# Windowed means as band matrices on TensorE behind the group's matrix, and token-major products in 512 columns

## The reference, cut to what matters

```python
def multiscale_pool_mixer(x, pool_w, pool_scale):     # POOL_WINDOWS = (2, 4, 8, 16), one for each group of 256 channels
    xg = x.astype(jnp.float32).reshape(B, S, POOL_GROUPS, POOL_CH)
    cs = jnp.cumsum(xg, axis=1)
    for gi, w in enumerate(POOL_WINDOWS):
        c = cs[:, :, gi]
        lagged = jnp.pad(c, ((0, 0), (w, 0), (0, 0)))[:, :S]
        mean = (c - lagged) / jnp.minimum(pos, float(w))[:, None]
        feats.append(mean - xg[:, :, gi])
    p = jnp.stack(feats, axis=2).astype(x.dtype)
    y = jnp.einsum('bsgc,gcd->bsgd', p, pool_w).reshape(B, S, D_MODEL)
    return y * pool_scale
# values of the linear attentions, of the memory attention and of the window attention
h = x @ w_in; i_v = split(h)            # (512 x 1024) @ (1024 x 512)
v = (mem_n @ w_v)                       # (256 x 1024) @ (1024 x 1024), in each of two layers
v = split(h2 @ w_in_2)                  # (512 x 1024) @ (1024 x 1024)
k, v = jnp.split(rmsnorm(h2, kv_norm) @ w_kv, 2, axis=-1)   # v: 128 columns, shared by all heads
```

## Time and profile before

| | us |
|---|---|
| median of 3 runs (lowest, highest) | 2575.34 (2572.87, 2576.18) |
| the profiled execution, its own time | 2575.22 |
| its span, first to last instruction | 2573.4 |
| PE busy | 2477.0 (96%) |
| DVE busy | 1482.1 (58%) |
| ACT busy | 879.1 (34%) |
| mean granted TensorE clock | 0.983 of 2.4 GHz |

### The profile page before, as it was taken

One profiled execution on the slowest core, in us unless ns is written; L12 is line 12 of the kernel. 1 busy time (PEld: TensorE's weight loads), 2 busy tenths in 40 slices (PEclk: granted clock), 3 DMA queues, 4 the chain that ended last, 5 costly groups with the idle time before them and its releaser, 6 DMA issues.

```text
span 2573.4 us, 29864 instructions
## 1 busy us (share of the span) xinstructions
PE 2477.0 (96%) x11776; PEld 2028.1 (79%) x11776; DVE 1482.1 (58%) x2044; ACT 879.1 (34%) x1184; POOL 9.9 (0%) x23
## 2 busy tenths in 40 slices
PE   8999999999999799999998999999999999999998
PEld 7898777788887577788886788778888777788886
DVE  6888645544446845544446535566666666566666
ACT  3444543422223543422224434322222455322222
POOL 0000000000000000000000000000000000000000
PEclk9998999999999799999999999999999999999999
DMA  5222211322222121222222220232222111222221
GB/s 189 82 83 82 99 66 66 115 95 91 93 96 89 58 82 66 82 98 98 96 91 80 82 99 33 68 117 96 98 98 98 66 66 50 91 92 96 97 98 65
DMA packets 32815, 225.56 MB, mean 88 GB/s; under 512 B 3765, under 2 KB 3813, under 8 KB 6368
## 3 DMA queue, kind: packets, MB, share of 16 engines
q1 hardware_dynamic: 31536, 220.21, 25.1%
q0 software_dynamic: 1200, 4.23, 0.5%
HBM read 222.30 MB, written 2.12 MB: 87 GB/s over the span
## 4 chain that ended last, share of the span: by engine, by line
PE 86%; DVE 8%; ACT 4%; issue 1%; DMA 0%; DVEq 0%; SPq 0%; ACTq 0%
PE bank L644 85%; DVE w_lo L1733 2%; ACT w_hi L1232 1%; ACT xs L1291 1%; DVE xs L1816 1%; DVE cacc L1924 1%; ACT xh L1245 1%; DVE hs L1975 0%; DVE xs L1830 0%; PE bank L1183 0%; DVE xs L1785 0%; DVE xl L1741 0%; DVE gs L1975 0%; PE bank L912 0%; DVE sum_x L1752 0%
## 5 line engine op out<-in xcount | busy, mean ns | idle before, releaser
L644 PE MATMUL bank<-xh,w_hi 128*128 128x512 f32 x1976 | 787.5, 399 | 58.0 <-DVE xl L1741 22.2
L644 PE MATMUL bank<-xl,w_hi 128*128 128x512 f32 x1976 | 777.2, 393 | 0.0
L644 PE MATMUL bank<-xh,w_lo 128*128 128x512 f32 x1976 | 776.9, 393 | 0.0
L1733 DVE TENSOR_TENSOR w_lo<-w_raw,w_hi 128x2048 fp32r<-128x2048 f32 x205 | 469.6, 2291 | 403.0 <-ACT w_hi L1232 402.4
L1232 ACT ACTIVATE w_hi<-w_raw 128x2048 fp32r<-128x2048 f32 x205 | 391.3, 1909 | 372.9 <-PE bank L644 372.7
L644 PEld LDWEIGHTS bank<-xh,w_hi 128*128 128x128 f32 x1976 | 375.9, 190 | 156.1 <-issue 34.8
L644 PEld LDWEIGHTS bank<-xh,w_lo 128*128 128x128 f32 x1976 | 375.6, 190 | 80.0
L644 PEld LDWEIGHTS bank<-xl,w_hi 128*128 128x128 f32 x1976 | 376.2, 190 | 78.7 <-issue 2.2
L1785 DVE TENSOR_TENSOR xs<-xs,bank 128x512 f32<-128x512 f32 x448 | 294.2, 683 | 116.3 <-PE bank L644 115.3
L644 PE MATMUL bank<-mhh,w_lo 128*128 128x512 f32 x512 | 199.2, 389 | 0.0
L644 PE MATMUL bank<-mhh,w_hi 128*128 128x512 f32 x512 | 199.2, 389 | 0.0
(11 more groups left out here) (282 smaller groups left out, 2688.2 us busy)
## 6 DMA issues: line engine op xcount, KB each, us to landing
w_raw<-weights_in SPq DMA_DIRECT2D x205, 1024.0 KB, 5.0
xs<-x_in SPq DMA_DIRECT2D x4, 512.0 KB, 8.0
sf<-rel_scratch POOLq DMA_DIRECT2D x1, 2048.0 KB, 11.7
y_out<-xs SPq DMA_DIRECT2D x8, 256.0 KB, 2.0
w_raw<-weights_in SPq DMA_DIRECT2D x2, 512.0 KB, 6.7
mk<-mem_in POOLq DMA_DIRECT2D x1, 1024.0 KB, 9.2
sum_q<-consts_in POOLq DMA_DIRECT2D x1, 256.0 KB, 9.4
scan<-consts_in POOLq DMA_DIRECT2D x1, 256.0 KB, 3.1
```

Source lines behind the costliest of these rows:

```text
L644: return pe.matmul(dst, a, b, start=start, stop=stop)
L1733: dve.tensor_tensor(w_lo[:, c % 2, :], w_raw[:, c % 2, :], w_hi[:, c % 2, :].bitcast(F32), ALU.subtract)\
```

## The change

1. **Pooling behind the matrix.** The windowed mean minus identity and the group's matrix commute. PE now multiplies first, token-major: `pool_values(g)` makes, from the split tiles of the group, 24 fp32r matmuls of 256 columns into two banks (`z`); ACT drains them to `zt`. `pool_means(g)` then makes for each of the group's two output tiles, in plain fp32, 4 matmuls of 128 columns (a tile of 128 tokens of `zt` stationary, a 128 x 128 band matrix streaming) and 3 of 16 columns for the window's reach over the next tile. The band matrices (`window`, 1152 columns of constants) replace `invpos`. DVE's `pool` and ACT's copies to `pa` go; DVE splits and evicts only. `mixn1`'s sums come from running sums on DVE in place of PE's ones-matmuls for six tiles.
2. **Token units in 512 columns.** `token_half` replaces `token_unit`: a unit holds 512 columns of half of the features, two units make a product. Each token tile has a bank of its own from the first half to the end of the second. This goes for `v`, `mv0`, `mv1a`, `mv1b`, `gv`. Drains come after the second half: the filler's at k = 4 alone.
3. **Statistics by token.** The one-column sums go. For `r0` PE transposes `rstd` by 4 matmuls against a column of the identity, behind `gq`'s second unit. For `r2` nothing is left: `sv` is made feature-major (24 matmuls of 512 columns), DVE multiplies it by `rstd` into `vf`, PE transposes it into bank 6 behind `sq`'s first unit, ACT drains it.

```diff
+    def token_pair(stage, p, tiles):
+        n = UNITS[stage] + 2 * p + 1
+        for t in range(tiles):
+            fill((stage, p, t), t if tiles == TT else 2 * (p % 2) + t, n if t == tiles - 1 else None)
...
+            def token_half(stage, p, half, src, tiles):
+                c = UNITS[stage] + 2 * p + half
+                pe.wait_ge(w_lo_ready, c + 1)
+                for t in range(tiles):
+                    key = (stage, p, t)
+                    if half == 0:
+                        wait_free(pe, key)
+                    for k in range(KT // 2):
+                        h, l = src(KT // 2 * half + k)
+                        last = mm3(bank(key)[:, :], (h[:, t * P:(t + 1) * P], l[:, t * P:(t + 1) * P]),
+                                   weights(c, k * T, T), half == 0 and k == 0, half == 1 and k == KT // 2 - 1)
+                    if half == 1:
+                        full(last, key)
+                if half == 0:
+                    last.then_inc(unit_used, 1)
...
+            def pool_values(g):
+                c = UNITS["pool"]
+                if g == 0:
+                    pe.wait_ge(w_lo_ready, c + 1)
+                for half in range(2):
+                    wait_free(pe, ("pool", "z", g, half))
+                for k in range(2):
+                    tile_ready(2 * g + k)
+                    h, l_ = xtile(2 * g + k)
+                    for half in range(2):
+                        key = ("pool", "z", g, half)
+                        for s in range(2):
+                            a = slice((2 * half + s) * P, (2 * half + s + 1) * P)
+                            last = mm3(bank(key)[:, s * 256:(s + 1) * 256], (h[:, a], l_[:, a]),
+                                       weights(c, (2 * g + k) * 256, 256), k == 0 and s == 0, k == 1 and s == 1)
+                        if k == 1:
+                            full(last, key)
+            def pool_means(g):
+                for half in range(2):
+                    wait_drained(pe, ("pool", "z", g, half))
+                for m in range(2):
+                    key = ("pool", 0, 2 * g + m)
+                    wait_free(pe, key)
+                    for t in range(TT):
+                        last = mm(bank(key)[:, t * P:(t + 1) * P], zt[:, g, t, m * P:(m + 1) * P],
+                                  window[:, 1 if t == 0 else 0, g, 0:P], True, t == 0)
+                        if t:
+                            last = mm(bank(key)[:, t * P:t * P + BAND - P], zt[:, g, t - 1, m * P:(m + 1) * P],
+                                      window[:, 0, g, P:BAND], False, True)
+                    full(last, key)
...
+                    pool_values(0)
+                    for g in range(4):
+                        if g < 3:
+                            pool_values(g + 1)
+                        pool_means(g)
+                    residual_norm("mixn1", [("pool", 0, m) for m in range(KT)])
...
@@ ACT, norm ffnn0 @@
+                    def between(k, copy_out):
+                        if k == 2:
+                            split_hi(n)
+                        if k == 4:
+                            copy_out(1)
+                            values_out(0)
+                        if k == 6:
+                            values_out(1)
+                    apply_norm("ffn", 0, high_of_xs, n - 2, FILLER["ffnn0"], between)
+                    split_hi(n + 1)
+                    scaled(0), scaled(1), values_out(2), scaled(2), scaled(3), pool_square(0), pool_square(1)
+                    values_out(3), scaled(4), scaled(5), pool_square(2), pool_square(3), scaled(6), scaled(7)
+                    for k in range(4, KT):
+                        pool_square(k)
@@ DVE, norm ffnn0: pool, pooled and their memsets go @@
+                    normalise("ffnn0", D, xs_at, KT, rest_of_xs, UNITS[FILLER["ffnn0"]], FILLER["ffnn0"], split_ahead=3)
...
@@ copy_out in apply_norm @@
-                        f = 512 * "ab".index(stage[3]) + 256 * j
-                        drain_pair(stage, j, lambda m: mv1[:, m * D + f:m * D + f + 256], MEM)
+                        f = 512 * "ab".index(stage[3])
+                        for t in range(MT * j):
+                            drain((stage, 0, t), mv1[:, t * D + f:t * D + f + T], bank((stage, 0, t))[:, :])
...
@@ PE, r0 and sv @@
+            wait_free(pe, ("r0", "tok"))
+            for t in range(TT):
+                last = mm(bank(("r0", "tok"))[:, t:t + 1], rstd[:, t * P:(t + 1) * P], ident[:, 0:1], True, True)
+            full(last, ("r0", "tok"))
...
+            for k in range(KT):
+                last = mm3(bank(("sv", 0, 0))[:, :], weights(c, k * P, P), ytile(k), k == 0, k == KT - 1)
...
             feature_unit("sq", 0, ready=tile_ready)
+            wait_drained(pe, ("sv", 0, 0))
+            wait_free(pe, ("svT", 0))
+            for t in range(TT):
+                a = slice(t * P, (t + 1) * P)
+                last = pe.transpose(bank(("svT", 0))[:, a], vf[:, a], ident[:, :])
+            full(last, ("svT", 0))
```

More of the change, by code:

```diff
@@ L171, in linear_attention @@
             fill((name, "kend", h), 5)
-            if filler:
+            if filler and filler[2 * h][0] == "mk0":
                 pair(*filler[2 * h])
+            elif filler:
+                token_pair("mv0", h - 2, MT)
             if h:
@@ L272, in plan_banks @@
         if l == 0:
-            pairs(FILLER["ffnn0"], 2)
+            token_pair(FILLER["ffnn0"], 0, MT)
     fill(("glr", 0, 0), 2 * (UNITS["glr"] % 2), UNITS["glr"])
@@ L736, in rms_norm_sums @@
                 squares_of_last(key)
[L737 to L741, removed]
-                        for m in range(SUMMED):
-                            last = mm(bank(tok)[:, t:t + 1], sq[:, m, a], ones[:, 0:1], False, m == SUMMED - 1)
-                    full(last, tok)
             def mem_src(k):
@@ L1589, in _, with values_out @@
-                    apply_norm("ffn", 0, pool_input, UNITS[FILLER["ffnn0"]], FILLER["ffnn0"])
-                    pooled(3)
-                    for k in range(KT):
+                    n = UNITS[FILLER["ffnn0"]] + 2
+                    seen.skip("tile_ready", POOL_TILES)
+                    def values_out(g):
+                        for half in range(2):
+                            key = ("pool", "z", g, half)
+                            drain(key, zt[:, g, 2 * half:2 * half + 2, :],
+                                  bank(key)[:, :].rearrange("p (t n) -> p t n", t=2))
@@ L1669, in _ @@
             split_hi(UNITS["sv"] + 1)
-            seen.next("rtok_ready")
-            key = ("sv", 0, 0)
-            wait_full(act, key)
-            for t in range(TT):
-                last = act.activation(vt[:, t * P:(t + 1) * P], bank(key)[:, t * P:(t + 1) * P], ACT.Copy, scale=rtok[:, t:t + 1])
-            free(last, key)
             def swa(it):
@@ L1705, in _ @@
             split_hi(UNITS["sq"] + 1)
+            drain(("svT", 0), vt[:, :], bank(("svT", 0))[:, :])
             for it in range(SWA_ITEMS + 2):
@@ L2238, in pooled @@
-                    def pooled(g):
-                        for k in (2 * g, 2 * g + 1):
-                            give(rest(k, pp[:, k, :]), "tile_ready")
-                    normalise("ffnn0", D, xs_at, KT, pool, UNITS[FILLER["ffnn0"]], FILLER["ffnn0"])
-                    pooled(3)
+                    normalise("ffnn0", D, xs_at, KT, rest_of_xs, UNITS[FILLER["ffnn0"]], FILLER["ffnn0"], split_ahead=3)
                     keys = [("pool", 0, m) for m in range(KT)]
```

252 lines of the change are left out of this document (108 added, 144 removed).

## The result

The changed kernel took 2556.41 us (median of 4 runs, 2556.38 to 2556.94) against 2574.6 for the kernel before beside it (4 runs): a ratio of 0.9927, 95% interval 0.9915 to 0.9939, or 18 us. Predicted were 2555 us, between 2548 and 2565. Five more runs of the same changed kernel, beside the last experiments, gave 2556.42 (2553.98 to 2556.58), ratio 0.9924 (0.9910 to 0.9937). The profiled execution took 2556.41 us, span 2554.6, mean granted clock 0.986.

A forecast was written before the change was run, and what follows sets the result against it. TensorE was taken as the bound, busy 96% of the span, so time goes only where its work or waits shrink. Terms -12.1 + 2.8 - 2.6 - 0.6 - 7.6 = -20.1 us, from 2575.22 to 2555, range 2548 to 2565.

The forecast's parts named there:

- Pooling mixer, -12.1: Norm `ffnn0` to `mixn1`'s mean: pooling moved from DVE to PE gains 12.1 us; bounds 14.6 gain, 6.9 loss.
- All three engines end together: End of the pooling mixer: ACT at about 869, PE at 870, DVE near 871 us.
- Price of a 16-column record, 0.10: Pooling means on PE: each fp32 record of 16 columns costs 0.10 us, between 0 and 0.122.
- Filler and first queries, +2.8: Behind `mixn1`: PE's first `xq1` queries wait for the `mv1b` drain, idle 5 us, clock lost; +2.8 us, bounds -0.5 and +9.
- `gv`, -2.6: `gv` unit: 192 pairs of 256-column records become single 512-column ones, 46.06 to 43.5 us, 2.6 us less.
- `v` and `mv0`, -0.6: Token units in 512 columns: `v` gives 0, as DVE ends later than PE; `mv0` gives 0.6 us.
- `r2` and `sv`, -7.6: At `sk`: one-column records go -2.6, clock -1.6, queries start earlier -4.6, transposes and bank wait +1.2; in all -7.6 us.
- without the narrow records I expect the full clock: -1.6: Right behind `r2`'s one-column records: nine 512-column matmuls return to full clock, 1.6 us less; bounds -1.8 and 0.
- `r0`, 0: At `r0`: 24 records go, but the next unit waits for DVE and 8 records return; 0, bounds -2.6 and +0.9.
- the first (clock kept in both gaps, 2550 us): Pooling mixer and `xq1` queries: PE keeps its clock in both new gaps; sum -25.1, 2550 us; chance 0.18.
- The second rival: Pooling mixer: engines wait more for one another, or narrow fp32 records cost the clock; 2561 to 2562 us; chance 0.18.
- The third (half clock throughout): Pooling products through filler and queries: PE stays at the lower clock; +13, 2588 us, slower than before; chance 0.04.

The follow-up runs named there:

- experiment 8: Changed kernel without the 24 matmuls of 16 columns (48 records) in the pooling means, a price only: no kernel time given, mixer 41.03 us in place of 41.86.
- experiment 9: Changed kernel with TensorE again summing tiles 0 to 5 for `mixn1` in place of VectorE's running sum: 2556.68 us, ratio 0.9931.
- wide alone: Also called experiment 2: kernel before with only the token units in 512 columns (`v`, `mv0`, `mv1a`, `mv1b`, `gv`): 2574.22 us, ratio 0.9996.
- Experiment 4: Changed kernel with `mv1b`'s two token tiles in banks 2 and 3 in place of 0 and 1: 2554.74 us.
- experiment 3: Kernel before with only the statistics by token and the shared values (no one-column sums, `sv` feature-major, four transposes): 2569.10 us, ratio 0.9980.
- Experiment 7: Changed kernel with `mv1b` in banks 2 and 3, the pool unit split one tile earlier, and the transposes in bank 3: 2550.97 us, ratio 0.9903.
- experiment 11: Changed kernel with four redundant copies of the mean on ScalarE in norm `cvn`, so everything later starts later: 2555.48 us.

## Why the prediction was right

The time, 2556.4 against 2555, came out because each large term was near its value. The clock effects that the prediction did not count cancelled in large part, and that is luck.

- **Pooling mixer, -12.1.** Measured -11.5 (53.3 to 41.9 us), alone -10.2. PE started at 842.35 where 0.7 us (DVE's later first tile) plus 841.6 had been expected, idle for 2.46 us (counted: 2.9), and lost its clock behind it. Right. The step "All three engines end together" was wrong: PE was done at 868.03 and waited 2.39 us for DVE's sums, and experiments 8 and 9 show that neither 4.6 us less work on PE nor fewer additions on DVE moves the end by more than 0.8 us. The clock's fall behind that wait, during the ones-matmuls, was not counted either.
- **Price of a 16-column record, 0.10.** Measured 0.096 (experiment 8).
- **Filler and first queries, +2.8.** Measured +2.5 (139.68 to 142.18); wide alone +2.2. The wait was 5.59 us, ended by ACT's `mv` drain, with 0.50 behind it. Experiment 4 takes back 2.0 of it by a bank number, which shows the cause.
- **`gv`, -2.6.** 46.06 to 43.47 us. The 1.5 us more in the attention behind it (54.56 to 53.04) are not the shorter drain: PE's two timelines there run level until 1605.9 us, and the difference comes where its clock fell in the kernel before, from 1606 us on.
- **`v` and `mv0`, -0.6.** Not to be told: without any edit to it the same stretch took 157.26 to 160.03 us. That `v` would give nothing fits the trace: the wait of PE behind it, 1.36 us before, is 2.51 us now.
- **`r2` and `sv`, -7.6.** The traces show -9.4, the instructions account for -6.2 (experiments 2 and 3). The removed records (-2.6), the unit on its later weights (-4.6) and transposes and bank wait (+1.2, the wait 0.78) sum to -6.0: these three were right. The clock gave 3.2 us where "without the narrow records I expect the full clock: -1.6" had been counted. Half of it, the low stretch right behind the records, is the counted term; it was gone in every trace without them, but in wide alone it was gone with them in place, so the records are a likely cause and not a proven one. The other half is the low stretch behind the 2.02 us gap ahead of `sk`. The prediction did not count it, and the second profile of the changed kernel (39.67 us) has it again: luck of the execution.
- **`r0`, 0.** From `ffnn1`'s mean to the last `gg` 119.29 and 119.27 us. Right, in sum.
- **What was not counted.** In stretches with the same instructions the clock cost the changed kernel 1.35 us up to `memn`, 1.1 in the first FFN, 1.5 in the first MLP and 2.9 in the second, 6.9 in all, and spared it 1.5 in the gated attention, 1.4 behind it and 1.6 at `sk` beyond what was counted, 4.5 in all. What is left is 2.4 us against the change. The counted terms, measured, come to -20.8 (with -1.4 for the whole stretch of `v` and `mv0`), with the 2.4 us to -18.4; the span fell by 18.8. Another pair of executions can come out otherwise: the runs of wide alone go from 2568.12 to 2576.25 us.

Of the rivals, the first (clock kept in both gaps, 2550 us) did not happen here. Experiment 7 came to it, 2551.0 us, by shorter gaps: PE kept 2.4 GHz behind 0.66 us of idleness in the mixer and 2.17 among the queries. Behind the second it might have fallen as well, as it did behind 2.13 in experiment 4. The second rival had a true half, the waits of DVE and ACT on one another at the mixer's end, and a false one, records of 16 columns that cost the clock: 842.35 to 868.03 was at half speed only right behind the gap. The third (half clock throughout) found no support.

## What to carry to other kernels

When a change moves results to fewer or longer-held banks, look up which unit next uses those banks and who drains them: here one bank number was worth 2 us of the gain. Before a difference is booked to an edit, look for the idle gaps of about 2 us near it in both traces: whether the clock fell behind them differs between executions of one kernel, at 1.1 to 1.6 us, or twice that, a time. And once an engine has been relieved, ask what the others do at the end of that stretch: 4.6 us less on PE brought 0.8.

## What the runs showed of the hardware

What the clock does behind a short idle gap of TensorE is not fixed. Gaps of the same length, between the same instructions, in the fourteen traces:

| gap ahead of | length, us | clock fell behind it |
|---|---|---|
| the last value products of the window attention | 1.93 | 5 of 14 |
| `sk` | 2.02 | 6 of 14 |
| the second MLP | 2.41 | 10 of 14 |
| the sums for `ffnn0` | 2.79 | 10 of 14 |
| the shorter ones, 31 in all (near 323, 463 and 907 us in the kernel before) | 1.68 to 1.73 | never |

Each idle gap of 4.1 us and more has a fall in it.

The clock also falls without such a gap, and what PE did there is narrow: the 24 records of one column at `r2` (2.60 us of them, PE busy throughout), records of 32 or 64 columns in the linear attentions (gaps under 0.9 us), and, in ten of eleven traces, eight matmuls that use 32 of the 128 rows (3.6 us) behind `r0`'s transposes. The one-column records at `r0` in the kernel before have 1.1 us of idleness behind them, and a fall behind that in all three traces that keep them. In none of the fourteen traces does a fall begin in the midst of longer runs of 512-column products on 128 rows: before each there is an idle gap or narrow work, at most 1.6 us back. (The start and the last microseconds of the kernel are left out of these counts.)

A fall is worth 1.1 to 1.6 us in such a stretch, or twice that, which is why a profile of a kernel of this length can't tell an edit of a microsecond by its span; the length of the edit's own stretch can, if the falls in it are counted. Why the same gap is followed by a fall in one execution and not in the next stays open. No run was made to tell it; the delay of experiment 11 and the two profiles of the changed kernel show only that the same instructions can go either way.

For the price of wide token units the Trainium skill ("TensorE: Matmul & The Clock Gate", Back-to-back issue gap) has 131 ns at 512 columns; `gv`'s 192 records took 43.47 us, 0.226 each, so the measurement decides against that figure for these fp32r products.
